# Gate and up products of two weight halves, interleaved tile by tile, in a two-block network on one core

## The reference, cut to what matters

```python
D_FF = -(-8 * D_MODEL // (3 * 256)) * 256      # 2816, and D_FF_2 = 2816

def swiglu(h, w_gu, w_down):
    u = h @ w_gu
    g, v = u[..., :D_FF], u[..., D_FF:]
    return (jax.nn.silu(g) * v) @ w_down

def swiglu_2(h, w_gate, w_up, w_down):
    return (jax.nn.silu(h @ w_gate) * (h @ w_up)) @ w_down
```

## Time and profile before

| | us |
|---|---|
| median of two runs | 1725.95 |
| the two runs | 1725.39 and 1726.51 |
| the profiled execution, first to last instruction (its span) | 1723.1 |
| PE busy | 1699.8 (99%) |
| PEld busy | 1596.8 (93%) |
| DVE busy | 1265.2 (73%) |
| ACT busy | 833.4 (48%) |
| POOL busy | 375.8 (22%) |
| granted TensorE clock, mean | 0.998 |

### The profile page before, as it was taken

How to read it: one execution, slowest core, us unless ns; L and a number is a source line. 1 busy time by engine, 2 the same in 40 slices (tenths; PEclk the granted TensorE clock), 3 DMA queues, 4 the chain that set the end, 5 groups by cost and what they waited for, 6 DMA issues and landing times.

```text
span 1723.1 us, 31820 instructions
## 1 busy us (share of the span) xinstructions
PE 1699.8 (99%) x12958; PEld 1596.8 (93%) x12958; DVE 1265.2 (73%) x1657; ACT 833.4 (48%) x1104; POOL 375.8 (22%) x425
## 2 busy tenths in 40 slices
PE   7999999999899999999999999999999999999999
PEld 7799999898789998999989999998999989999997
DVE  7898889786868889798757876666666665676663
ACT  5875444444655444444453255444444435554442
POOL 0222012535404223600032140002100128330000
PEclk9999999999999999999999999999999999999999
DMA  8246567685106777565646445464445544335560
GB/s 318 106 150 210 197 221 256 228 303 181 58 13 221 249 272 263 180 203 178 229 154 232 150 148 192 173 225 164 167 175 210 205 155 160 124 134 193 194 228 33
DMA packets 50711, 321.02 MB, mean 186 GB/s; under 512 B 7696, under 2 KB 8912, under 8 KB 20144
## 3 DMA queue, kind: packets, MB, share of 16 engines
q1 hardware_dynamic: 36432, 280.61, 46.0%
q0 software_dynamic: 12736, 36.87, 6.6%
q10 hardware_dynamic: 1440, 2.10, 0.3%
HBM read 307.39 MB, written 10.09 MB: 184 GB/s over the span
## 4 chain that ended last, share of the span: by engine, by line
PE 96%; DVE 2%; ACT 1%; issue 1%; DMA 0%; ACTq 0%
PE bank L2285 19%; PE bank L2286 19%; PE bank L2287 19%; PE bank L2291 18%; PE bank L2292 9%; PE bank L2464 1%; PE bank L2572 1%; PE bank L2939 1%; PE bank L2891 1%; PE bank L2646 1%; PE bank L2757 1%; PE bank L2582 1%; PE bank L2533 1%; PE bank L2534 1%; PE bank L2535 1%; PE bank L2477 1%
## 5 line engine op out<-in xcount | busy, mean ns | idle before, releaser
L1459 DVE TENSOR_TENSOR w_lo<-raw,w_hi 128x1024 fp32r<-128x1024 f32 (+2 forms) x486 | 643.6, 1327 | 270.6 <-ACT w_hi L1029 269.3
L1029 ACT ACTIVATE w_hi<-raw 128x1024 fp32r<-128x1024 f32 (+2 forms) x486 | 538.3, 1115 | 576.2 <-PE bank L2287 346.1
L2285 PE MATMUL bank<-hg_hi,w_hi 128*128 128x256 f32 x2648 | 754.3, 285 | 11.3 <-DVE hg_lo L1464 10.4
L2286 PE MATMUL bank<-hg_lo,w_hi 128*128 128x256 f32 x2648 | 750.3, 283 | 0.0
L2287 PE MATMUL bank<-hg_hi,w_lo 128*128 128x256 f32 x2648 | 750.2, 283 | 0.0
L2285 PEld LDWEIGHTS bank<-hg_hi,w_hi 128*128 128x128 f32 x2648 | 509.0, 192 | 16.0 <-DVE w_lo L1459 10.8
L2286 PEld LDWEIGHTS bank<-hg_lo,w_hi 128*128 128x128 f32 x2648 | 509.2, 192 | 0.2
L2287 PEld LDWEIGHTS bank<-hg_hi,w_lo 128*128 128x128 f32 x2648 | 509.2, 192 | 0.0
L2291 PE MATMUL bank<-hid,w_hi 128*128 128x512 f32 x1056 | 372.9, 397 | 0.0
L2292 PE MATMUL bank<-hid,w_lo 128*128 128x256 f32 x1056 | 296.3, 281 | 0.0
L2291 PEld LDWEIGHTS bank<-hid,w_hi 128*128 128x128 f32 x1056 | 198.5, 188 | 48.2 <-issue 1.0
(11 more groups left out here) (412 smaller groups left out, 1909.0 us busy)
## 6 DMA issues: line engine op xcount, KB each, us to landing
raw<-in_w SPq DMA_DIRECT2D x189, 1024.0 KB, 4.9
raw<-in_w SPq DMA_DIRECT2D x48, 1408.0 KB, 6.4
raw<-in_w SPq DMA_DIRECT2D x8, 768.0 KB, 5.4
b_rows<-in_s_b_rows POOLq DMA_DIRECT2D x8, 512.0 KB, 7.6
l_rows<-s_powers POOLq DMA_DIRECT2D x64, 64.0 KB, 8.5
s_ca<-cp_s POOLq DMA_DIRECT2D x8, 512.0 KB, 4.5
s_ba<-ba_s POOLq DMA_DIRECT2D x8, 512.0 KB, 7.4
ba_slot<-s_ba POOLq DMA_DIRECT2D x8, 512.0 KB, 5.2
```

What stands on the lines that cost most here:

```text
L1029: act.activation(w_hi[s][:, 0:n], raw[r][:, c * n:(c + 1) * n], ACT.Copy).then_inc(hi_made, 1)
L1459: dve.tensor_tensor(w_lo[s][:, 0:n], raw[r][:, c * n:(c + 1) * n], w_hi[s][:, 0:n].bitcast(F32), ALU.subtract).then_inc(lo_made, 1)
L2285: pe.matmul(psum, w_hi_ap, x_hi_ap, start=first, stop=False, **kw)
L2286: pe.matmul(psum, w_hi_ap, x_lo_ap, start=False, stop=False, **kw)
```

## The change

`side_by_side` takes both halves of a side at once. For each of the eight tiles it issues w_hi x hg_hi for the first half and then for the second, the same for w_hi x hg_lo, and the same for w_lo x hg_hi: 48 products, whose targets alternate between the two 256-column parts of one bank. It waits for the splits of both halves before the first product, and adds 2 to `half_used` behind the last. The flag `start` stands at the very first product alone. It is used for every side of every pair but the first side of pair 0, in all six feed-forward phases.

```diff
+            def side_by_side(half, psum, it=0):
+
+                weights(half, it)
+                sides = [(weights(half + c, it), psum[:, c * T:(c + 1) * T]) for c in range(2)]
+                for k in range(KT):
+                    w = slice(k * P, (k + 1) * P)
+                    for (hi, lo), out_ap in sides:
+                        pe.matmul(out_ap, hi[:, w], hg_hi[:, k, :], start=k == 0 and out_ap is sides[0][1], stop=False, skip_group_check=True)
+                    for (hi, lo), out_ap in sides:
+                        pe.matmul(out_ap, hi[:, w], hg_lo[:, k, :], start=False, stop=False, skip_group_check=True)
+                    for (hi, lo), out_ap in sides:
+                        last = pe.matmul(out_ap, lo[:, w], hg_hi[:, k, :], start=False, stop=k == KT - 1, skip_group_check=True)
+                last.then_inc(half_used, 2)
...
                         if p == 0 and side == 0:
                             two_from_hg(half, [psum[:, 0:T], bank[FIRST_BANK["ffn"]][:, T:2 * T]], ph["hg"])
                         else:
-                            for c in range(2):
-                                from_hg(half + 2 * side + c, psum[:, c * T:(c + 1) * T], it)
+                            side_by_side(half + 2 * side, psum, it)
```

## The result

The changed kernel takes 1750.49 us (median of two runs, 1749.79 to 1751.19) against 1725.95: 1.0134 times as long, 95% interval 1.0097 to 1.0171. The forecast was 1752. The profiled execution spans 1749.3 us, 26.2 more than before.

The account below looks back on a forecast made before the run. PE bounds the kernel (96% of the chain); its 120 ns pace was to stay. Stalls from coarser release and demand, 24.57 us, plus 1.4 of restarts make 26 on 1725.95: 1752 us, range 1726 to 1768.

Parts of the forecast that it names:

- The bound of 2 ns: Gate and up products: operand placement might shift the 120 ns pace 2 ns either way, 12 us over 6048 products.
- Rival A: Gate and up products: the new order frees the pace from 120 ns; 1707 us, 1.1% faster; chance 10%.
- Rival B: Gate and up products: time per product rises with tiles read twice beside alternating buffers; 1764 us at 122 ns; chance 15%.
- pair 0: Each feed-forward phase: h+5 is split only behind norm's reciprocal and scaled gate, so PE waits 1.36 us at pair 1.
- output weights behind pairs 3 and 6: Second phase: the inserted output-weights steps delay DVE's splits, stalling PE 3.06 us together.
- input weights behind pair 1: Second phase: the inserted input-weights step stalls PE 0.28 us, being 0.91 less 0.63 already held up.
- down projection: Second phase, behind pair 9: first down half, longer to split, comes 0.3 us late.
- pair 0 and closing: Third phase: first block closed before h+7's split, usable 2.83 us after PE begins pair 1's up side; pair 0's wait included.
- four angles steps: Third phase: each inserted angles step on DVE stalls PE 1.43 us, 5.72 together.
- Y: DVE: time from hid_lo's start through an inserted step to the next split; 5.01 us for output weights; stall Y - 3.48.
- a few tenths at most: Before the down projection: pair 10's hid_lo ends close to when it is wanted; wait allowed six times, within the range.
- Rival C: Splits and buffers: coarser release is free, its waits hidden by something misjudged; unchanged at 1726 us; chance 9%.

Follow-up runs that it names:

- experiment 1: Kernel before's order (one half after the other), but both halves of a side waited for and given back together: 1752.77 us, 1.0165.
- experiment 2: Changed kernel with the products of both halves adding onto the same columns, so no neighbours have different targets: 1750.55 us, 1.0168.
- the release alone: Kernel before, each half still waited for by itself, but both halves of a side given back together at its end: 1726.36 us, 1.0009.
- Experiment 3: Kernel before with one part each: waiting for both halves before the side, 1735.10 us, 1.0059; giving both back together at its end, 1726.36 us, 1.0009.
- the quick placement: Kernel before with hg 32, weight buffers 96 and the rest 128 bytes further on in SBUF: 1686.13 us, 0.9766.
- experiment 6: Kernel before with hg, weight buffers and what follows moved 32 to 128 bytes, four ways: 1716.02, 1725.91, 1686.13, 1714.82 us; changed kernel moved once: 1743.38 us.
- experiment 7: Changed kernel with hg 32, weight buffers 96 and the rest 128 bytes further on: 1725.91 us, 1.0016.
- experiment 5: Changed kernel with h+5's split moved ahead of the norm's reciprocal and scaled gate on DVE, in pair 0 of each phase only: 1748.05 us, 1.0128.
- experiment 4: Changed kernel with both splits of every side put ahead of DVE's other work in that side: 1765.32 us, 1.0242.

## Why the prediction was right

**The pace.** Taken as unchanged from the 31 half ends that already had different targets: 120.0 before and after, in experiments 1 and 2, and 113.3 in both orders in the other placement. The bound of 2 ns for "the new order pairs other addresses" wasn't needed. Rival A (a freed pace) falls: the changed kernel kept 120.0, and experiment 2 has the new order without different targets and the same time. Rival B (a slower pace) falls with the row of 120.0. The Trainium skill's 26.3 ns for each of the 126 saved counts ("TensorE: Matmul & The Clock Gate", "The cost: per-tile semaphore tail"), which the page fitted on small tiles packed into the array, do not show: the release alone, which saves as many, is no faster than the kernel before (1.0009). The Trainium skill's 109 ns for a product of this size (same page, "Back-to-back issue gap"), which the page gives for a single gap with no time for the weight load in it, was reached by no placement; the quickest gave 113.3.

**The stalls**, from start to start less 0.12, us:

| phase | what | expected | measured |
|---|---|---|---|
| 1 | pair 0 | 1.36 | 1.37 |
| 1 | chains behind pairs 1 and 6 | 1.33, 1.33 | 1.43, 1.25 |
| 1 | output weights behind pair 8 | 1.53 | 1.61 |
| 2 | pair 0 | 1.36 | 1.37 |
| 2 | output weights behind pair 0, less 0.26 of before | 0.37 | 0.29 |
| 2 | input weights behind pair 1 | 0.28 | 0 |
| 2 | output weights behind pairs 3 and 6 | 3.06 | 3.60 |
| 2 | down projection | 0.3 | 1.58 in three |
| 3 | pair 0 and closing | 2.83 | 2.68 |
| 3 | four angles steps | 5.72 | 5.44 |
| 3 | closing in pair 9 | 1.02 | 0.99 |
| 4 to 6 | pair 0 | 4.08 | 3.83 |
| | sum | 24.57 | 25.4 |

With 0.07 for each of 21 restarts the measured stalls give 26.9. From the first of these phases on, the changed kernel's profiled execution grew by 27.2 us; the stretch before it, which the change does not touch, happened to be 1.1 shorter, and the span grew by 26.2. So it is luck in part that the span agrees with the 26 of the sum to 0.2: the sum is about 1 us short, and the shorter stretch hides that. The medians differ by 24.5.

**Where terms were off.** Three, all in the second phase, and they add to 1.5 us; the terms of the last four phases were 0.7 too high. The step behind pairs 3 and 6 also holds an instruction that I had left out of Y, on DVE in the changed kernel:

```profile
585.94 0.68 DVE L1636 TENSOR_TENSOR hid<-hid_f,hid 128x512 fp32r<-128x512 f32 x1
...
590.94 0.34 DVE L1586 SCALAR_TENSOR_TENSOR k_sb<-s_par,vec,bank 128x128 f32<-128x128 f32 x1
591.20 1.22 DVE L1459 TENSOR_TENSOR w_lo<-raw,w_hi 128x1024 fp32r<-128x1024 f32 x1
```

hid_lo to the next split 5.26 us for the 5.01 of pair 0. Behind pair 1 PE had 16 products of the S5 preparation to do ahead of pair 3, 0.57 us and their surroundings, which covered the 0.28. And at the down projection, "a few tenths at most" in the range, PE waited for `w_lo` and twice for others:

```profile
667.29 0.50 PE L2291 MATMUL bank<-hid,w_hi 128*128 128x512 f32 x1 [0.28 <-DVE w_lo L1459]
...
675.03 0.50 PE L2291 MATMUL bank<-hid,w_hi 128*128 128x512 f32 x1 [0.40 <-DVE hid L1636]
```

The second row is the wait for pair 10's hid_lo. From start to start the two are 0.44 and 0.57. A third, of 0.57 as well, comes later in the same projection, ended by `h`, and no term of the prediction stands for it. Experiment 3 has the first two in full with the release alone, so they belong to it, and of the third 0.30. The "few tenths" for hid_lo were allowed in all six phases and came in this one.

**Rival C** (the release is hidden) falls: the 21.2 us of idle time ended by `w_lo`, and experiment 1, where the coarser wait and release alone bring them.

**What isn't shown.** Why the distance in SBUF goes with the pace, whether it is the distance that acts or something else that moved with it, and whether 64 modulo 128 is the best there is: five placements were run in the old order (the kernel before and four moved ones), at four distances, and all four moved hid and hq as well. The down products were at 233.9 and 118.3 ns in the kernel before and at 233.0 and 116.8 in the quick placement, counted from start to start.

## What to carry to other kernels

Before interleaving accumulation groups to spare the array, look at the places where the stream already changes its target: if the step is the same there, the interleaved order has nothing to win at those places; here it was free and bought nothing. Then price what the interleaving does to the buffers: wanting two together and giving two back together costs a buffer of lead at each end, and here the two together cost much more than the sum of each alone (26 us for 10 and 1). When the pace of the same products differs between stages, try moving the operands before you reorder the products: here 64 bytes of distance were worth 2.3%, and the best kernel of this study is the old order with hg 32 and the weight buffers 96 bytes further on, 1686.13 us.

## What was not expected of the hardware

- The pace of products with a 128x128 weight load each and 256 moving columns went with the distance of moving operand and weights in SBUF modulo 128 bytes: 120.0 ns at 0, 118.7 and 118.3 at 96 and 32, 113.3 at 64 (experiments 6 and 7).
- Adding onto the neighbour's PSUM columns costs nothing: 120.0 ns with and without, and 113.3 with and without in the quick placement.
- Single stalls of PE inside a dense stream were followed, in some cases and not in others, by a few microseconds at the lower granted clock (in experiment 5, 19 products where 28 is usual). It fell behind idle times from 1.74 us (experiment 6, the changed kernel moved) to 2.85 us (experiment 4), and did not fall behind one of 2.09 us in experiment 7. In the changed kernel, whose stalls in these phases have at most 1.66 us of idle time, it fell behind none of them. Of experiment 7, behind 2.28 us of idle time and behind 2.09 (busy time and count of PE, PEclk):

```profile
590.90:594.30 3.40, 3.40 (x19) 0.50 0.86 314
261.60:265.00 3.40, 3.40 (x30) 1.00 0.97 309
```
